# Seven-product blocks written as running sums: four ScalarE copies and two VectorE additions in place of one copy and five additions

## The reference

```
h = rmsnorm_3(x, norm1_w)
rq, rk, rv, rg, mq, mk, mv, ga, gb = split(h @ w_in)
a = (silu(rg) * retention(rotary(rq), rotary(rk), rv)) @ w_ret_out
b = moba_attention(rmsnorm_3(mq), rmsnorm_3(mk), mv) @ w_moba_out
x = x + (sigmoid(ga) * a + sigmoid(gb) * b) @ w_o
h2 = rmsnorm_3(x, norm2_w)
x = x + (silu(h2 @ w_ffn_gate) * (h2 @ w_ffn_up)) @ w_ffn_down
```

## Time and profile before

| what | value |
| --- | --- |
| median of three runs | 1971.0 us (1969.97 to 1972.1) |
| span of the profiled execution | 1967.1 us |
| TensorE busy | 1954.6 us, 99% |
| VectorE busy | 1194.6 us, 61% |
| GpSimd busy | 1119.2 us, 57% |
| ScalarE busy | 402.2 us, 20% |
| read from memory | 294.35 MB, 150 GB/s over the span |

### The profile page before, as it was taken

How to read it: one execution, slowest core, us unless ns; L and a number is a source line. 1 busy time by engine, 2 the same in 40 slices (tenths; PEclk the granted TensorE clock), 3 DMA queues, 4 the chain that set the end, 5 groups by cost and what they waited for, 6 DMA issues and landing times. The chain is left out here.

```text
span 1967.1 us, 37363 instructions
## 1 busy us (share of the span) xinstructions
PE 1954.6 (99%) x14834; PEld 1848.6 (94%) x14834; DVE 1194.6 (61%) x3033; ACT 402.2 (20%) x978; POOL 1119.2 (57%) x750
## 2 busy tenths in 40 slices
PE   9999999999999999999999999999999999999999
PEld 7788889999899999999999899999999999999998
DVE  4244535989978477524888987667713487554541
ACT  2241521111321222110111222222102025220000
POOL 1000038785176588758678155487776674448783
PEclk9999999999999999999999999999999999999999
DMA  5313445444444454445444343454444442445544
GB/s 212 134 43 132 150 151 179 160 164 139 149 144 143 156 174 167 171 148 172 168 159 168 121 162 131 150 172 172 167 164 161 136 147 97 140 150 172 172 161 140
DMA packets 44267, 299.76 MB, mean 152 GB/s; under 512 B 5440, under 2 KB 6592, under 8 KB 10176
## 3 DMA queue, kind: packets, MB, share of 16 engines
q1 hardware_dynamic: 42560, 295.42, 43.7%
q10 hardware_dynamic: 1536, 1.97, 0.3%
HBM read 294.35 MB, written 1.05 MB: 150 GB/s over the span
## 5 line engine op out<-in xcount | busy, mean ns | idle before, releaser
L712 PE MATMUL bank<-arena,ring 128*128 128x128 f32 (+2 forms) x3854 | 603.4, 310 | 1.2 <-ACT arena L1344 0.6
L712 PEld LDWEIGHTS bank<-arena,ring 128*128 128x128 f32 x3854 | 540.4, 191 | 43.6 <-ACT arena L1344 3.1
L712 PE MATMUL bank<-xn,ring 128*128 128x128 f32 (+3 forms) x3104 | 467.8, 306 | 0.0
L712 PEld LDWEIGHTS bank<-xn,ring 128*128 128x128 f32 (+1 forms) x3104 | 424.4, 191 | 31.1 <-issue 4.4
L712 PE MATMUL bank<-arena 128*128 128x128 f32 (+3 forms) x3048 | 391.5, 284 | 0.0
L712 PEld LDWEIGHTS bank<-arena 128*128 128x128 f32 (+1 forms) x3048 | 364.9, 192 | 9.3 <-issue 1.5
L712 PE MATMUL bank<-arena,h_res 128*128 128x128 f32 x2696 | 322.4, 276 | 2.1 <-POOL h_res L1802 1.2
L712 PEld LDWEIGHTS bank<-arena,h_res 128*128 128x128 f32 x2696 | 310.6, 192 | 5.1 <-POOL h_res L1802 2.4
L1798 POOL TENSOR_TENSOR arena<-ring 128x1024 f32<-128x1024 f32 (+1 forms) x103 | 243.0, 2360 | 124.7 <-DMA ring<-wstream 124.2
L1798 POOL TENSOR_TENSOR h_res<-ring 128x1024 f32<-128x1024 f32 (+1 forms) x95 | 221.7, 2334 | 127.1 <-DMA ring<-wstream 111.9
L1849 DVE SCALAR_TENSOR_TENSOR bank<-arena,par,bank 128x256 f32<-128x256 f32 x640 | 259.5, 483 | 15.3 <-DVE arena L2265 7.7
(11 more groups left out here) (241 smaller groups left out, 1805.0 us busy)
## 6 DMA issues: line engine op xcount, KB each, us to landing
ring<-wstream SPq DMA_DIRECT2D x264, 1024.0 KB, 4.8
ring<-wstream SPq DMA_DIRECT2D x16, 768.0 KB, 4.2
cst<-consts SPq DMA_DIRECT2D x1, 2488.0 KB, 14.7
h_res<-tokens SPq DMA_DIRECT2D x2, 544.0 KB, 5.1
arena<-arena ACTq DMA_DIRECT2D x16, 64.0 KB, 3.4
out<-arena SPq DMA_DIRECT2D x4, 256.0 KB, 5.4
arena<-arena ACTq DMA_DIRECT2D x28, 32.0 KB, 3.1
ring<-wstream SPq DMA_DIRECT2D x2, 288.0 KB, 2.9
```

What stands on the lines that cost most here:

```text
L712: return pe.matmul(o, lhs, rhs, start=start, stop=stop, skip_group_check=True)
```

## The change

179 of the 214 blocks get a new form, `chain_block`. The 35 others (the parts `down`, and the first block of `attn` in L0 and L1) keep the old one, now named `down_block` or as they were.

- **Order of the products.** w11 into c22, w21 into c11, m0 into c12, m2 onto c22, m3 into c21, w22 onto c12, m1 onto c22. The slot is released after the sixth product, and the raw quarter w22 is read by it.
- **Running sums.** Partial results stay in the banks, and ScalarE copies them out at four moments, into `snaps` (a copy called s1 after the first product, s5 after the third, s2 after the fifth, s3 after the seventh). The fourth product waits for s1, the sixth for s5, the seventh for s2, since each adds to what has been copied. `snaps` has two places, used in turn.
- **Joining.** VectorE makes two additions of 256 columns, one after the sixth product and s2, one after s3; the second frees both banks. `take_pair` lets a block's two banks be claimed together, and all eight banks are one tensor now, so that one addition reads two of them.
- **GpSimd.** In the first block after a norm the sums come in the order m0, m2, m3, m1, all from raw quarters and what is there, so m1 last.
- **SyncE** waits for the last sum that reads the slot (`spent`), whichever it is.
- **ScalarE's other work** stands between two of the copies: in most stages between s2 and s3 of the block, in the head turns the softmax between s5 and s2.
- The arena shrinks from 31000 to 30976 columns a partition.

The diff, cut to its core:

```diff
-                pe.wait_ge(*e.landed(slot))
-                claim("x")
-                product("x", 0, w[:, 0], lambda k: plain(0, k, 0), opens=True)
-                product("x", 2, w[:, 3], lambda k: plain(1, k, 0))
-                pe.wait_ge(*e.at((sums, "sum", 3)))
-                product("x", 1, w[:, 2], ...).then_inc(*e.done(f"slot_done{slot}", ...))
-                claim("y")
-                pe.wait_ge(*e.at(("mix1", block)))
-                product("y", 1, m[:, 0], ...)
...
+            def chain_block(block, plain, sums, ready=None, token_major=False):
...
+                product("c22", w[:, 0], lambda k: plain(0, k, 0), opens=True).then_inc(*e.done("main_done", ("pe", (block, "p1"))))
+                product("c11", w[:, 3], lambda k: plain(1, k, 0), opens=True)
+                pe.wait_ge(*e.at((sums, "sum", 0)))
+                pe.wait_ge(*e.at(("mix1", block)))
+                product("c12", m[:, 0], lambda k: sums_at_k(sums, 0, k)).then_inc(*e.done("main_done", ("pe", (block, "p5"))))
+                pe.wait_ge(*e.at((block, "s1")))
+                pe.wait_ge(*e.at((sums, "sum", 1)))
+                pe.wait_ge(*e.at(("mix2", block)))
+                product("c22", m[:, 2], lambda k: sums_at_k(sums, 1, k))
+                pe.wait_ge(*e.at(("mixed", block)))
+                product("c21", m[:, 3], lambda k: plain(1, k, 1)).then_inc(*e.done("main_done", ("pe", (block, "p4"))))
+                pe.wait_ge(*e.at((block, "s5")))
+                pe.wait_ge(*e.at((sums, "sum", 3)))
+                product("c12", w[:, 2], lambda k: sums_at_k(sums, 3, k)).then_inc(*e.done(f"slot_done{slot}", ("pe", (block, "p3"))))
+                pe.wait_ge(*e.at((block, "s2")))
+                pe.wait_ge(*e.at((sums, "sum", 2)))
+                pe.wait_ge(*e.at(("mix1b", block)))
+                product("c22", m[:, 1], lambda k: sums_at_k(sums, 2, k)).then_inc(*e.done("main_done", ("pe", (block, "t"))))
...
-            def heads(L, pr, pts, out, gates=None, beside=None):
+            def heads(L, pr, pts, out, block_of, meanwhile=None, beside=None):
                 for h in range(9):
                     if h < 8:
+                        snapshot(block_of(h), 1)
+                        snapshot(block_of(h), 5)
                         softmax(L, h, pr)
+                        snapshot(block_of(h), 2)
+                        if meanwhile:
+                            meanwhile(h)
+                        snapshot(block_of(h), 3)
...
+            def snapshot(key, n):
+
+                done, of, to = {1: ("p1", "c22", "c11"), 5: ("p5", "c12", "c22"), 2: ("p4", "c22", "c12"), 3: ("t", "c22", "c21")}[n]
+                (half, col), at = part_at[of], snap_at[to]
+                if n == 1 and snap_before(key):
+                    act.wait_ge(*e.at((snap_before(key), "c22")))
+                act.wait_ge(*e.at(("pe", (key, done))))
+                act.activation(snap(key)[:, at:at + P], psum[e.bank_of((key, half))][:, col:col + P],
+                               ACT.Copy).then_inc(*e.step((key, f"s{n}")))
...
+                    dve.wait_ge(*e.at((key, "s2")))
+                    dve.wait_ge(*e.at(("pe", (key, "p3"))))
+                    dve.tensor_tensor(view[:, :, 0, :], half("x"), kept[:, :, 0, :], ALU.add).then_inc(*e.step((key, "c12")))
+                    dve.wait_ge(*e.at((key, "s3")))
+                    dve.tensor_tensor(view[:, :, 1, :], half("y"), kept[:, :, 1, :], ALU.add).then_inc(*e.frees((key, "x"), (key, "c11")))
```

More of the change, by code:

```diff
@@ L774, in out_product, with down_block @@
                     halves(stage, q, 8, [P, P], rhs, T, ready=None if q else ready, split=None if q else split)
-            def fast_block(block, key, plain, sums, first=True, last=True, held=None, ready=None, token_major=False):
+            def down_block(block, key, plain, sums, first, last, held, ready):
                 slot, n = e.next_block(), pairs_of(block)
@@ L817, in fast_block, with product @@
                 return banks
+            def chain_block(block, plain, sums, ready=None, token_major=False):
+                slot = e.next_block()
+                w = ring[:, slot, :].rearrange("p (s k c) -> p s k c", s=4, c=P)
+                m = mixed_of(block).rearrange("p (s k c) -> p s k c", s=4, c=P)
+                def product(place, weight, act, opens=False):
+                    half, col = part_at[place]
+                    for k in range(4):
+                        one, two = (act(k), weight[:, k, :]) if token_major else (weight[:, k, :], act(k))
+                        ins = mm(bank[half], slice(0, P), slice(col, col + P), one, two, opens and k == 0, k == 3)
+                    return ins
+                pe.wait_ge(*e.landed(slot))
+                bank, emptied = e.take_pair(block)
+                for when in emptied:
+                    pe.wait_ge(*when)
+                for event in ready or ():
+                    pe.wait_ge(*e.at(event))
+                product("c22", w[:, 0], lambda k: plain(0, k, 0), opens=True).then_inc(*e.done("main_done", ("pe", (block, "p1"))))
[16 more added lines that the diff above has]
+                product("c22", m[:, 1], lambda k: sums_at_k(sums, 2, k)).then_inc(*e.done("main_done", ("pe", (block, "t"))))
@@ L860, in late_stage @@
                 for it in range(1, 4):
-                    fast_block((L, part, it, 0), (L, part, it, 0), plain, sums)
+                    chain_block((L, part, it, 0), plain, sums)
             def of_tokens(buf):
```

258 lines of the change are left out of this document (154 added, 104 removed).

## The result

The changed kernel takes 2009.3 us in the median (2005.9 to 2011.2) against 1970.5 for the kernel before, a ratio of 1.0196 with a 95% interval of 1.0182 to 1.0211. It is slower by 38.8 us, where 21 were forecast; the range of 1974 to 2008 ends 1.3 us too early.

A forecast was written before the change was run, and what follows sets the result against it. TensorE, busy 1954.6 of 1967.1 us, bounds the kernel, so relieving other engines pays nothing by itself. New waits of 6.9 + 2.4 + 6.5 + 3.4 + 2.5 - 0.7 = 21.0 us on 1971.0 give 1992.0, range 1974 to 2008.

The forecast's parts named there:

- (a): Four places where successive blocks share destination h_res: products wait for GpSimd's sums, 1.73 us each, 6.9 us.
- (b): Six first blocks after a norm, where GpSimd waits for VectorE's activation sums: 0.4 us each, 2.4 us.
- (c): Nine loads over 5.6 us in back to back blocks, no longer hidden: 0.2 to 1.8 us each, 6.5 us.
- (d): Second block after ordinary products, slot free late anyway, plus slower mixes in tight stretches: 3.4 us, bounds 1 and 7.
- margin lost: Rival: copies reach TensorE 0.1 to 0.3 us later, costing each of 179 blocks: 2008 to 2028, chance 0.10.
- ScalarE behind something else: Last eight head turns of the third layer: softmax delays the third copy, four turns, 2.5 us, bounds 0 and 6.
- A gain: Transposes wait less for VectorE's scaling: -0.7 us; scaling's collision with GpSimd (589.26), some 4 us, left to the range.
- The clock: Rival: longer waits drop the clock to 1.2 GHz, the two pairs of (a) adding some 25 us: 2017, chance 0.02.
- Its signs: Afterwards: load issued 5.5 us into blocks, some 50 sum waits, copy waits only in last head turns, other blocks 6.25.

The follow-up runs named there:

- four repairs: The changed kernel with v's own home, norm work between copies, w22 fifth outside head turns, and GpSimd's order m0, m2, m3, m1 in all new blocks: 1977.7 us.
- the last kernel: The kernel with four repairs, with the old block form in the 24 head-turn blocks: 1970.5 us, ratio 0.9999 to the kernel before.

## Why the prediction was right or wrong

**Right in sign, and in the mechanism for about half of the loss.** That what VectorE is spared is worth nothing, that plain blocks stay at 6.25 us, and that a signal costs where it comes close to its due time: all this is in the rows above. The places (a) to (d) lost 20.1 us in the trace, where 19.2 were forecast; of the other 22.3 us the sum had 1.8.

**Term by term.** (a) 6.9 us forecast, 6.9 in the trace, 6.1 back in the experiment. (b) 2.4, and 2.7. (c) 6.5, and 8.1, within its bounds of 0 and 10. (d) 3.4, and 2.4. The rival "margin lost" did not come, and the margin worked out, 0.2 us, was measured at 0.25. That (c) and (d) came near in sum owes something to luck, since in the other traces some of the late loads fall on other blocks. (The 3.7 us of cover named under (c) are 3.5 by its own rows; nothing hangs on it.)

**The first step that failed** is the paragraph "ScalarE behind something else". It looked only for work that stands ahead of a copy, and so makes the copy late. It didn't look for work that stands behind the last copy. Copy s3 pins ScalarE to the end of each block, where p1 let it go on after 3.2 us; at three places a table load and sixteen operations stood behind it, the first of which TensorE wanted at once. 11.9 us in the trace and 12.4 in the experiment against 0 in the sum: by the medians this alone explains two thirds of the 17.8 us that the forecast lacked.

**The second is a size.** The head turns were put at 2.5 us, and "A gain" set 0.7 against that and left the collision with GpSimd to the range, as "some 4 us". They lost 9.6. The four late turns of C that the term names lost 4.0; L0 and L1, for which the sum had nothing but the gain, lost 5.0. The turns were costed from the times of VectorE's maxima in the trace of before, which holds GpSimd's sums where they were; the same text had the sums move by 2.7 us against the block. Two statements of the prediction were never put together. It even named the row that shows the price (589.26) and its reason: by the Trainium skill (SBUF, State Buffer: "SBUF: two separate sides") the engine that starts first keeps the other off the shared ports for its whole instruction. The trace agrees with 2.29 us for two operations on one column. But it applied it to the scaling only, not to the maxima, the sums of activations and all else that VectorE does from tile to tile. Nor were these 4 us in its bounds: as given they add up to 2002.6 us, where it says 2004, and to 2006.6 with them, which only the wider range to 2008 takes in.

**The gain of 0.7 us** didn't show: TensorE waits for the scaling 1.8 us in all, where it waited 2.1.

**The clock** was given a chance of 0.02, for the places of (a). There it stayed full. It fell elsewhere (below), for 1.3 us in the profiled run.

**Its signs.** The load is issued 5.55 us into the block, as it said. Waits for ScalarE's copies were to come only in the last head turns; two of the longest, 2.5 and 2.2 us, came in the first turns of L0 and L1.

Put together: 21.0, with 11.9 for the norms, 7.8 for the head turns, 1.6 for the loads, 0.3 for (b), 0.5 at the start and less 1.0 for (d), is 42.1, beside 42.4 in the trace. The medians differ by 3.6 us less: the run profiled was 1.9 over its median, and only 1.8 us lay around its span, where the prediction had 3.9.

## What to carry to other kernels

When an engine gets a step at the end of a stage that it had at its start, read what stands behind it on that engine as well as what stands ahead of it: a table load and the first work of the next stage that were free are free no longer. When a change moves an engine's work in time, take no duration of the engine beside it from the old trace without asking what it will now stand beside. And a step that is released later is paid for by due times: a reordering of GpSimd's four sums, with the same work, gave back 13.7 of 38.8 us.

## What the runs showed of the hardware

**A stop can bring the clock down afterwards.** Stretches of the kernel after around the stop behind L0 o (us, then for each engine busy time and instructions; the column PEclk is the granted clock):

```profile
674.00:677.00 3.00, 3.00 (x8) 2.10 (x7) 0.00 (x0) 2.81 (x8) 2.72 (x4) 0.50 0.00 0
677.00:683.00 6.00, 6.00 (x29) 5.27 (x29) 0.81 (x1) 0.47 (x1) 0.00 (x0) 1.00 0.01 3
```

TensorE had stood for 2.4 us and then run with small waits when the clock was granted at 0.50, the lower level of 1.2 GHz, for 3 us. The same stop of 2.4 us in L1 and C brought no such stretch in this run; that is the difference of 4.8 to 3.5 us in the table. In the kernel with a home of its own for v the mean clock was 0.83 over 550 to 560 us and 0.72 over 1174 to 1180 and over 1784 to 1790, at stops that had not brought it down in the changed kernel's run. The profiled runs have one such stretch in the changed kernel and with s2 copied twice, four with s2 ahead of the softmax and with w22 fifth, two or three in five other kernels, and none in the kernel before, in that with the slot released late, with the norm work between the copies, with four repairs and in the last kernel (the last 10 us of the program left out). At the stops behind part o a stretch goes with 0.6 to 1.3 us more than the 3.53 us of a stop without one. So the same stop costs about 1 us more in one run than in another, and a repair that takes such a stop away can give this back as well. The runs of the changed kernel lie 5.3 us apart and those with s2 ahead of the softmax 7.8, where eighteen runs of the kernel before lie within 2.7. In the changed kernel the clock does not explain it, since the fastest and the slowest run have the same mean clock, 0.999; with s2 ahead of the softmax it falls from 0.998 in the fastest run to 0.996 in the slowest. How much the loads add wasn't separated.

**Two engines on one memory.** In the rows above an operation of VectorE from tile to tile that meets a sum of GpSimd ends only after that sum has ended. Two operations on one column took 2.29 us. Of the four sums of 512 columns in the kernel with the late release, each ended 0.54 or 0.55 us after the sum of GpSimd beside it (726.10 + 2.35 = 728.45, and 726.15 + 2.85 = 729.00), and took 1.64 to 2.85 us where one alone takes 0.69. GpSimd pays too: its sums of 512 columns took 1.60 us there and 1.27 elsewhere. Instructions of half the length on GpSimd took 1.0 us off the stop in each of the two first turns.
